# Expert blocks of 32 rows, and attention scores over 64 partitions each: one change to a two-block transformer kernel

## The reference, cut to what matters

```
s = jnp.einsum('bqgnd,bgqjd->bgnqj', qb, k_sel) * scale      # d = 64
p = masked_softmax(s, mask_s)
```

```
def expert_block(args):
    xb, e = args
    hg, hu = jnp.split(xb @ w_gu[e], 2, axis=-1)     # 1024 -> 2 x 512
    return (jax.nn.silu(hg) * hu) @ w_down[e]        # 512 -> 1024
```

## Time and profile before

| | |
|---|---|
| median of 3 runs | 3789.73 us (3787.17 to 3801.17) |
| the profiled execution's own time | 3786.93 us |
| its span in the profile | 3785.1 us |
| PE busy | 3227.8 us, 85% of the span |
| ACT, DVE, POOL busy | 1002.7, 1270.8, 399.6 us |
| bytes moved | 669.66 MB, 177 GB/s over the span |

### The profile page before, as it was taken

The page is one execution under the profiler, slowest core; times in us unless marked ns, Lnnn a source line. Parts: engine busy times, 40 slices in busy tenths (PEclk is TensorE's granted clock), DMA queues, the critical chain, the costliest instruction groups (busy, mean ns, idle before and its releaser), DMA issues. The chain is left out here.

```text
span 3785.1 us, 47531 instructions
## 1 busy us (share of the span) xinstructions
PE 3227.8 (85%) x18903; PEld 2025.2 (54%) x18903; DVE 1270.8 (34%) x1922; ACT 1002.7 (26%) x1668; POOL 399.6 (11%) x543
## 2 busy tenths in 40 slices
PE   7987989999896999989787877896897986878985
PEld 5765667878664688777452222232466863322332
DVE  3343434332546433222731100012595553100112
ACT  2333422221334221122621111111342332111212
POOL 1012310000302000000000000001121230000002
PEclk9989999999998999999888988998898998989997
DMA  7335323332411332322058999973113126999996
GB/s 194 82 113 205 140 52 93 100 94 61 107 34 53 84 94 82 107 78 82 31 207 327 390 391 395 393 288 92 39 50 78 39 57 257 388 394 390 385 388 242
DMA packets 442385, 669.66 MB, mean 177 GB/s; under 512 B 86709, under 2 KB 310882, under 8 KB 440938
## 3 DMA queue, kind: packets, MB, share of 16 engines
q1 hardware_dynamic: 416121, 601.45, 45.8%
q0 software_dynamic: 11936, 34.85, 3.1%
q10 hardware_dynamic: 14160, 30.94, 2.2%
HBM read 632.03 MB, written 35.13 MB: 176 GB/s over the span
## 5 line engine op out<-in xcount | busy, mean ns | idle before, releaser
L1834 PE MATMUL moe_ps<-moe_wgu,moe_xbT 128*64 128x512 f32 x2496 | 601.1, 638 | 120.1 <-DMA moe_wdn<-in_moe_w_down 119.0
L1834 PEld LDWEIGHTS moe_ps<-moe_wgu,moe_xbT 128*64 128x64 f32 x2496 | 189.5, 147 | 523.4 <-issue 522.0
L1845 PE MATMUL moe_ps<-moe_wdn,moe_hT 128*64 128x512 f32 x1248 | 285.0, 598 | 36.9 <-ACT moe_hT L1901 36.9
L181 PE MATMUL ffn_in_ps<-ffn_xhi,ffn_in_whi 128*128 128x512 f32 x704 | 280.6, 399 | 14.0 <-DVE ffn_xlo L323 14.0
L182 PE MATMUL ffn_in_ps<-ffn_xlo,ffn_in_whi 128*128 128x512 f32 x704 | 280.2, 398 | 0.0
L183 PE MATMUL ffn_in_ps<-ffn_xhi,ffn_in_wlo 128*128 128x512 f32 x704 | 280.0, 398 | 0.0
L2008 DVE TENSOR_TENSOR moe_gated_h<-moe_gated_h,moe_ps 128x256 f32<-128x256 f32 x78 | 32.8, 421 | 686.2 <-ACT moe_gated_h L1898 686.2
L1898 ACT ACT_TABLE_LOAD x78 | 100.1, 1283 | 475.3 <-issue 475.3
L1845 PEld LDWEIGHTS moe_ps<-moe_wdn,moe_hT 128*64 128x64 f32 x1248 | 82.7, 136 | 189.1 <-issue 133.6
L2012 DVE COPY moe_y<-moe_ps 128x512 f32<-128x512 f32 x78 | 54.0, 692 | 345.2 <-PE moe_ps L1845 345.2
L181 PEld LDWEIGHTS ffn_in_ps<-ffn_xhi,ffn_in_whi 128*128 128x128 f32 x704 | 133.4, 190 | 48.0 <-issue 15.6
(11 more groups left out here) (675 smaller groups left out, 5948.5 us busy)
## 6 DMA issues: line engine op xcount, KB each, us to landing
moe_wgu<-in_moe_w_gu SPq DMA_DIRECT2D x64, 4096.0 KB, 31.6
moe_wdn<-in_moe_w_down SPq DMA_DIRECT2D x64, 2048.0 KB, 31.5
ffn_came<-in_ffn_w_in SPq DMA_DIRECT2D x88, 512.0 KB, 5.0
na_modw<-in_ada_w SPq DMA_DIRECT2D x10, 4096.0 KB, 12.5
expert_rows<-moe_y ACTq DMA_DIRECT2D x156, 128.0 KB, 6.1
da_in_w<-in_attn_w_qkv SPq DMA_DIRECT2D x12, 1024.0 KB, 5.2
ro_w<-in_rw_w_rkv SPq DMA_DIRECT2D x24, 512.0 KB, 4.0
ffn_came<-in_ffn_w_out SPq DMA_DIRECT2D x8, 1408.0 KB, 7.3
```

The source lines that it names most:

```text
L181: nc.tensor.matmul(ps[0:width, slot * tiles + o], whi[:, slot, k, cols], xhi[:, k], start=(k == 0), stop=False)
L1834: last = nc.tensor.matmul(psGU[q * BLK:(q + 1) * BLK], xbT[:, k], cols[:, q], start=(k == 0), stop=(k == KD - 1))
L1845: last = nc.tensor.matmul(psY[q * BLK:(q + 1) * BLK], hT[:, k % 2, (k // 2) * BLK:(k // 2 + 1) * BLK], wdn[:, s, k, q * 512:(q + 1) * 512] ...
```

## The change

1. BLK becomes 32. A block's rows come as quarters: 128 partitions gather 1 KB each from a row-shuffled copy of x, so that DVE's transposes of 32 x 32 squares turn `xg` into `xbT` without PE. Gathers and stores are double-buffered (`xg`, `y`), and POOL, ACT and DVE walk blocks in pairs, so an odd count is padded with one idle block.
2. Gate and up are made in two halves (`a`) of 64 hidden columns for each of four column groups: 32 matmuls of 32 x 128 in a half, four side by side, read from the weights in runs of 32 floats. Each half is followed at once by silu, product and a DVE transpose; PE no longer transposes h, and ACT no longer copies `xbT` or `hT`.
3. The down product is 16 matmuls of 32 x 256, four side by side. ACT, not DVE, copies it out, and issues four stores of 32 rows of 1 KB.
4. The routing's tail is rewritten: block and place come from shifts and masks of integers instead of comparisons with thresholds. x is stored in four transfers instead of eight.
5. The first mixer's keys lie once in `kz`, written by four instructions of 128 partitions; its scores are matmuls over 64 partitions, both heads before both masks.

```diff
@@ nsa
-                    for h in range(2):
-                        half = slice(h * HD, (h + 1) * HD)
-                        last = nc.vector.scalar_tensor_tensor(out=kz[half, b, a, h], in0=projT[half, t], scalar=B.cols("k_gain", 1 + b, 1)[half],
-                                                              in1=psD[half, u % 4], op0=ALU.mult, op1=ALU.mult)
-                    last.then_inc(scaled, 1)
+                    nc.vector.scalar_tensor_tensor(out=kz[:, b, a], in0=projT[:, t], scalar=B.cols("k_gain", 1 + b, 1), in1=psD[:, u % 4],
+                                                   op0=ALU.mult, op1=ALU.mult).then_inc(scaled, 1)
@@ nsa_attention, scores
                 for h in range(2):
-                    nc.tensor.matmul(psS[:, v % 2, h, 0:n], projT[:, it, i * P:(i + 1) * P], kz[:, b, it // 4, h, 0:n], start=True, stop=False)
+                    half = slice(h * HD, (h + 1) * HD)
+                    nc.tensor.matmul(psS[:, v % 2, h, 0:n], projT[half, it, i * P:(i + 1) * P], kz[half, b, it // 4, 0:n], start=True, stop=False)
+                for h in range(2):
                     last = nc.tensor.matmul(psS[:, v % 2, h, i * P:n], B.ident_b[:], B.causal_b[:], start=False, stop=True)
@@ norm_moe
-BLK = 64
+BLK = 32
+            def each_pair(eng, body):
+                pairs = (block_count(eng) + 1) >> 1
+                body(0, 0, 0)
+                body(1, 1, 0)
+                with eng.Fori(1, pairs) as j:
+                    body(j * 2, 0, j)
+                    body(j * 2 + 1, 1, j)
+                return pairs
@@ sync
-                    sp.wait_ge(gu_done, end)
+                    sp.wait_ge(gu_done[1], end)
@@ gpsimd
+                def gather(b, s, j, spare=None):
+                    if not (isinstance(b, int) and b < 2):
+                        pool.wait_ge(gathered[s], j * 16)
+                        pool.wait_ge(x_ready, b)
...
+                    nc.gpsimd.indirect_dma_start(out=xg[:, s], out_offset=None, in_=x_dram.rearrange("s (g n) -> (s g) n", g=4),
+                                                 in_offset=bass.IndirectOffsetOnAxis(ap=pick_ids[:, s:s + 1].bitcast(U32), axis=0)).then_inc(gathered[s], 16)
@@ tensor
-                def turn_x(b):
...
                 def expert_block(b, s):
-                    pe.wait_ge(b_taken, (b + 1) * 2)
-                    for k in range(KD):
-                        cols = wgu[:, s, k].rearrange("p (g q n) -> p q g n", g=2, q=2)
-                        for q in range(2):
-                            last = nc.tensor.matmul(psGU[q * BLK:(q + 1) * BLK], xbT[:, k], cols[:, q], start=(k == 0), stop=(k == KD - 1))
-                    last.then_inc(gu_done, 1)
-                    turn_x(b + 1)
-                    pe.wait_ge(h_ready, b + 1)
...
+                    pe.wait_ge(x_ready, b + 2)
+                    for a in range(2):
+                        for k in range(KD):
+                            cols = wgu[:, s, k].rearrange("p (g a m j i) -> p a j g m i", g=2, a=2, m=2, j=4)[:, a]
+                            for j in range(4):
+                                last = nc.tensor.matmul(psGU[j * BLK:(j + 1) * BLK, a], xbT[:, k], cols[:, j], start=(k == 0), stop=(k == KD - 1))
+                        last.then_inc(gu_done[a], 1)
                     pe.wait_ge(y_taken, b + 1)
                     for k in range(KH):
-                        for q in range(2):
...
+                        if k % 2 == 0:
+                            pe.wait_ge(h_ready, b * 2 + k // 2 + 1)
+                        for j in range(4):
+                            last = nc.tensor.matmul(psY[j * BLK:(j + 1) * BLK], hT[:, k * BLK:(k + 1) * BLK], wdn[:, s, k, j * 256:(j + 1) * 256],
+                                                    start=(k == 0), stop=(k == KH - 1))
@@ scalar
+                def gate_and_store(b, s, j):
+                    for a in range(2):
+                        act.wait_ge(gu_done[a], b + 1)
+                        nc.scalar.activation(gated[:, a], psGU[:, a, 0:HD], ACT.Silu).then_inc(silu_done, 1)
+                    act.wait_ge(down_done, b + 1)
+                    if not (isinstance(b, int) and b < 2):
+                        act.wait_ge(y_stored[s], j * 64)
+                    nc.scalar.activation(y[:, s], psY, ACT.Copy).then_inc(y_taken, 1)
                     act.wait_ge(y_taken, b + 2)
...
+                    for q in range(4):
+                        rows = y_dram[:, q * 256:(q + 1) * 256].rearrange("(b t) n -> t b n", t=BLK)[:, bass.ds(b, 1)].rearrange("t o n -> t (o n)")
+                        act.dma_start(rows, y[q * BLK:(q + 1) * BLK, s]).then_inc(y_stored[s], 16)
@@ vector
+                def turn_x(s, j):
+                    dve.wait_ge(gathered[s], j * 16 + 16)
+                    V.transpose(scratch[:, 0:KD * BLK], xg[:, s]).then_inc(x_ready, 1)
+
+                def gate_and_turn(b, s, j):
+                    for a in range(2):
+                        dve.wait_ge(silu_done, b * 2 + a + 1)
+                        V.tensor_tensor(h[:, a], gated[:, a], psGU[:, a, HD:P], ALU.mult).then_inc(h_made, 1)
+                        dve.wait_ge(h_made, b * 2 + a + 1)
+                        V.transpose(hT[:, a * HD:(a + 1) * HD], h[:, a]).then_inc(h_ready, 1)
+                    turn_x(1 - s, j + s)
```

More of the change, by code:

```diff
@@ L581, in clear @@
                     nc.gpsimd.tensor_copy(sel[:, h, a], B.ident[:, h * HD:(h + 1) * HD])
-            for T in (kz, kcz, vcz):
+            for T in (kcz, vcz):
                 nc.gpsimd.memset(T[:], 0.0)
@@ L1645 @@
 HID = D // 2
-BLK = 64
+BLK = 32
 MAXB = EXPERTS + 2 * SEQ // BLK
+ROOM = MAXB + 4
 SLOTS = 3
@@ L1684, in norm_moe @@
             e32 = sb(s2, "e32", [P, 4, EXPERTS])
-            over = sb(s2, "over", [P, EXPERTS, SEQ // BLK - 1])
+            blocks = sb(s2, "blocks", [P, EXPERTS], I32)
             ahead = sb(s2, "ahead", [P, TC, EXPERTS])
@@ L1688, in norm_moe @@
             destf = sb(s2, "destf", [P, 2 * TC])
[L1689 to L1692, removed]
-            slot_hot = sb(s2, "slot_hot", [P, 2 * TC, BLK])
[L1694 to L1700, removed]
-            sq = (y[:], xbT[:].rearrange("p k t -> p (k t)"))
-            rstd = gated_h[:].rearrange("p g n -> p (g n)")
-            LT = xg[0:GROUPS + EXPERTS, 0:SEQ]
+            place = sb(s2, "place", [P, 2, 2 * TC], I32)
+            placef = sb(s2, "placef", [P, 2, 2 * TC])
+            quarter = sb(s2, "quarter", [P, 1], I32)
+            quarterf = sb(s2, "quarterf", [P, 1])
+            hot = sb(s2, "hot", [P, 2 * TC, MAXB + 2])
+            slot_hot = sb(s2, "slot_hot", [P, 2 * TC, BLK])
+            xg = sb(s2, "xg", [P, 2, D // 4])
+            LT = sb(s2, "LT", [GROUPS + EXPERTS, SEQ])
+            pick_ids = sb(s2, "pick_ids", [P, 2], I32)
+            scratch = sb(s2, "scratch", [P, D])
+            xbT = scratch[:, 0:KD * BLK].rearrange("p (k t) -> p k t", t=BLK)
+            hT = scratch[:, KD * BLK:KD * BLK + P]
+            gated, h = (scratch[:, c:c + P].rearrange("p (a n) -> p a n", a=2) for c in (D // 2, D // 2 + P))
+            y = sb(s2, "y", [P, 2, D // 4])
+            sq = (y[:].rearrange("p s n -> p (s n)"), scratch[:, 0:SEQ])
+            rstd = scratch[:, SEQ:2 * SEQ]
             ps = s2.enter_context(nc.psum_tensor(N + "ps", [P, 8, 512], F32))
@@ L1818, in _ @@
                 for u in range(2 * TC):
-                    last = nc.tensor.matmul(psI[0:BLK, 0:MAXB + 1], slot_hot[:, u], hot[:, u], start=(u == 0), stop=(u == 2 * TC - 1))
+                    for g in range(4):
+                        last = nc.tensor.matmul(psI[g * BLK:(g + 1) * BLK, 0:MAXB + 2], slot_hot[:, u], hot[:, u], start=(u == 0), stop=(u == 2 * TC - 1))
                 last.then_inc(ids_summed, 1)
-                def turn_x(b):
-                    pe.wait_ge(gathered, (b + 1) * 16)
-                    pe.sem_inc(turn_begun, 1)
-                    for k in range(KD):
-                        last = nc.tensor.transpose(psX[:, k // 4, (k % 4) * BLK:(k % 4 + 1) * BLK], xg[:, k * P:(k + 1) * P], B.ident[0:BLK, 0:BLK])
-                    last.then_inc(b_turned, 1)
@@ L1856, in expert @@
                         expert_block(b, s)
-                    return end
                 for e in range(EXPERTS):
                     expert(0 if e == 0 else end_of(pe, e - 1), e, e % SLOTS, e // SLOTS)
+                pe.wait_ge(down_done, end_of(pe, EXPERTS - 1))
+                pe.sem_inc(gu_done[0], 1)
+                pe.sem_inc(gu_done[1], 1)
+                pe.sem_inc(down_done, 1)
             @block.scalar
```

128 lines of the change are left out of this document (47 added, 81 removed).

## The result

The changed kernel takes 3643.7 us (median of 4 runs, 3635.0 to 3649.6) where the kernel before, beside it, takes 3795.5: a ratio of 0.960, 95% interval 0.957 to 0.963. A second measurement gave 0.963 (0.962 to 0.965).

The account below looks back on a forecast made before the run. Weight loads bound most expert blocks, PE the first stage's last 13 and the first attention. Terms -14 attention, -2 ahead of it, -42 and -10 expert stages, -1 routing sum to -69: 3718, median 3720 us, range 3685 to 3765.

Parts of the forecast that it names:

- the two stages' streams: Weight loads in both expert stages: less block traffic saves 11.4 us in the first and 6.9 in the second.
- the prediction's own counts of blocks: Blocks run while weights load: 25 and 35 before, 26 and 47 after, in the first and second expert stage.
- The attention: First attention: shorter scores, seen where PE does not wait, save 14 us, bounds 6 and 23.
- PE's price: Expert blocks of 32 rows on PE: a floor of 5.4 us a block, with the drains.
- ACT's wrong by two terms: Expert blocks on ACT: 7.0 us with a table load, every second block, else 5.4; issuing four stores takes 2.4.
- Experts 26 to 31: PE-bound tail of the first expert stage: 21 blocks at a mean of 6.2 us take 130, plus 2.5 for low clock.
- The second stage: Second expert stage: 10 us less, from earlier last weights and a shorter last block, less a longer end.
- The last block: Second expert stage, block behind the last weights: 8.2 us instead of 12.7, including 2.5 for PE's low clock.
- Gathers did not become the limit: Rival, expert stages: gathers needing 14 us make a block 7.8 us, total about 3757; chance 12%.
- rival 1.34: Rival, expert stages: traffic priced by packets stays 1.34 us a block, total also 3757; chance 11%.
- Four column groups: Slower rival, expert products: groups run only two at a time, 10.6 us a block, total 3833; chance 8%.
- Routing: Routing in both expert stages: rewritten vector operations and transposes save 1 us, bounds -3 and +3.

Follow-up runs that it names:

- the edit alone: Kernel before with only the attention's part of the change, experts as before: ratio 0.9999.
- the filler: Changed kernel plus ten unread PE products at the wait for the second modulation load in three attention rounds: ratio 0.961.
- after_best: Changed kernel plus the ten unread products, with PE keeping an expert's end in its register as the next begin: 3640.0 us, ratio 0.961.
- before_both: Kernel before, 64-row blocks kept, with wgu at a multiple of 512 bytes and gathers as 128 pieces over 128 partitions: 3722.0 us, ratio 0.981.
- after_again: The changed kernel itself measured once more, unaltered: 3650.3 us, ratio 0.963.

## Why the prediction was wrong, point by point

**The step that failed** is "6.29 MB and a block's gather and stores (64 x 4 KB and 128 x 2 KB, 0.52 MB) at 391 GB/s are 16.1 + 1.34 = 17.4 us". The sum fits the spacing of 17.34 and both parts are wrong. In the undisturbed window the weights ran at 409 GB/s, so an expert's took 15.4 us, and the block's traffic the other 1.96. The DMA view before, between the issues of experts 3 and 31 of the second stage (3207.89 to 3694.55 us, traffic of 34 blocks), divides it:

```profile
q0 software_dynamic: 2720, 8.92, 6.6%
q10 hardware_dynamic: 5440, 8.92, 4.8%
```

The stores take 4.8% of 486.7 us, 0.7 us a block, the gather's own packets 0.9, and the 0.3 left is what the weights beside it lose. So the gather costs 1.3 us; by the two windows above it is 72 packets of weights lost and 64 of its own, 10 ns of the stream each, 1.4. So the traffic that could be removed was half as large again as its bytes at the mean rate. The weights themselves I took as fixed, and they gained 0.4 us an expert from 64 bytes of another tile. Forecast for the two stages' streams: 18 us; measured by issue of the loads: 35.3 + 45.1 = 80.4. With 1.96 us a block before, 0.75 after and 0.4 an expert, the prediction's own counts of blocks would have given 39 and 45. The mean of the earlier trace rows was a mixture, and the trace of before had the pure rate one window earlier.

The rows put the gather at 1.3 to 1.4 us of the stream. The Trainium skill, "SBUF — State Buffer", section "Door 1: The DMA port swizzle (why `[64,N]` ≈ `[32,N]`)", says that partitions 0 to 63 lie behind only 8 of the 16 ports that DMA writes through, at 218 GB/s; by this an estimate is 262 KB / 218 = 1.2 us. The runs agree, with 1.3 to 1.4 and with 408 GB/s for 324 over 128 partitions, and the prediction should have weighed this rule.

On the address, the Trainium skill, "DMA: Bandwidth & Descriptors", section "How a descriptor splits into AXI transactions", says of reading that a descriptor which does not start at a multiple of 256 bytes fetches, and pays for, the bytes below its start. The section says nothing of the side that is written, which is the one moved here. Carried over to that side, its count is 134 beats for 128 for 4096 bytes from 192, an estimate of 4.7%. The direction agrees, and 420/409 = 2.7% decides the size. Only these two starts were tried.

**The attention: forecast 14, got 0.** The price of the scores of 384 keys was right. The timeline of PE after (against the earlier trace rows):

```profile
457.86 0.92 PE L884 MATMUL na_psS<-nsa_kz,nsa_projT 64*128 64x384 f32 x4
...
458.83 0.61 PE L907 MATMUL na_psT<-ident,na_prob 128*128 128x128 f32 x4
```

That is 0.97 us, as in the earlier trace rows. Where it is seen was wrong. In a round without paired loads I had 2.6 us seen and 0.6 back as waits. PE's wait for POOL grew from 22.2 to:

```profile
PE na_psT L907 <- POOL na_prob L1093: 30.6, 35, 1.7
PE na_psC L940 <- DMA na_modw<-in_ada_w: 22.5, 3, 8.3
```

10 waits more and 8.4 us, a good 1 a round: a round gained 1.1, not 2.0. In the three paired rounds I had a gain of 1.3 each and got a loss of 0.6 to 3.8 (the edit alone: 3.0, 1.0 and a gain of 0.3), with PE idle longer before the load and granted a lower clock behind it (0.79 to 0.85 for 0.92); the filler gave the clock back and, in two of three, the time. The 0.97 us is what rows 8 take; the Trainium skill, "TensorEngine Tiling (Array Packing)", section "Key Properties", says that a change of the tiling mode drains TensorE, and nothing shows here on top of it.

**The block of 32 rows.** PE's price (5.4 forecast, 5.44 to 5.5 measured) was right, ACT's wrong by two terms: no table load in the loop, since the first pair is written out ahead of it and leaves the silu's table loaded, and stores issued in 1.75 us instead of 2.4. What I had not priced is 1.0 us at each change of expert: between the last product issued and the next, PE spends 0.8 to 1.2 us where it spends 0.2 between two blocks of one expert, and the trace has two loads of a register of 0.3 us each there; with one of them gone, in after_best, it is 0.6.

With the table load put back, blocks near the forecast's appear. The load stands 0.36 us behind the last issue of stores and the ACTIVATE 0.02 us behind the load; the Trainium skill, "ScalarE: Activation LUTs", section "What ACT_TABLE_LOAD costs", adds a drain of 1.38 us to a switch, and there is no room for it on either side. Experts 26 to 31 took 123.7 us for 132.5 forecast, but 130 to 132 in five other profiles. So this term came out nearly right in size by luck: the forecast had a table load in every second block, and what the other profiles have in its place are changes of expert and PE's slower pace (last section).

**The second stage**: the stream again, 45 of its 59 us. The last block, in the timeline of PE:

```profile
3592.91 3.70 PE L1841 MATMUL moe_ps<-moe_wgu,moe_scratch 128*32 128x128 f32 x128 [1.61 <-DMA moe_wdn<-in_moe_w_down]
...
3596.43 2.13 PE L1848 MATMUL moe_ps<-moe_wdn,moe_scratch 128*32 128x256 f32 x32
```

It took 5.7 us (forecast 8.2): PE had waited 1.6 us before it, not long, and gate and up took the 3.7 us of the full clock. The idle block and the four stores cost 2.7 us (forecast 4.2).

**The rivals.** Gathers did not become the limit: in the last blocks (2407 to 2518 us) PE's products of gate and up wait for nothing but issue. Packets of the stores are cheap: a block of 32 rows left 15.73 - 6.29 MB/420 GB/s = 0.75 us of traffic (forecast 0.85, rival 1.34). They are also fewer than the 256 of 1 KB that I counted: the trace has 128 of 1 KB for the stores, 46 ns each, but 32 of 4 KB for the gather, 160 ns each, together 0.7 us over 16 engines. Four column groups do run together in runs of 32 floats, 29 ns an instruction.

**Routing** gave 5.0 us for 1. Not all of it is the rewritten tail: before_both, which has the old one, gave 3.1 of it (57.3 + 59.0 us for 58.6 + 60.8). The rest is open.

**The range.** Its bounds added up are 3682 to 3781, not 3685 to 3765. The measured 3643.7 lies below either, because no bound let the weights load faster, or the traffic before have cost more than its bytes.

## What to carry to other kernels

Split a mean bandwidth before pricing with it: time the same transfer where nothing else moves, and see what is left for the rest; a sum that fits may be made of two wrong parts. Look where in SBUF a stream lands, both the partitions of what shares the queue and the start address of its own tile: the two were worth 71 us here without any block of 32 rows, half of what the whole change gave, and cost a reshaped gather and 64 bytes. The issue of a load tells when its slot came free, not when its bytes moved: between experts 10 and 20 the issues are 15.7 us apart both in before_both and in the changed kernel, while the weights' queue moved 60.8 MB in the one and 63.0 in the other. An edit that shortens PE's work ahead of a wait for a transfer gives it to the wait, and here it came with a lower clock that took more.

## What the runs showed of the hardware that was not expected

- A start of 192 bytes past a multiple of 256 costs each 4 KB row of a load 3%: 409 against 420 GB/s, both ways.
- A gather of 64 rows of 4 KB into 64 partitions holds all 16 DMA engines at 324 GB/s while it lasts; as 128 pieces of 2 KB over 128 partitions it leaves them at 408.
- The same blocks of 32 rows go through PE at two paces. In the profile of the change they are 5.5 us apart; in that of after_again most are 6.0, with a stop of 0.2 us within gate and up, and on both sides of it the instructions are slower, 34 and 31 ns for 29:

```profile
2427.75 1.69 PE L1841 MATMUL moe_ps<-moe_wgu,moe_scratch 128*32 128x128 f32 x50
2429.64 2.31 PE L1841 MATMUL moe_ps<-moe_wgu,moe_scratch 128*32 128x128 f32 x75 [0.20 <-issue]
```

What stops it was not settled; PE waits there for nothing that the profile shows.
